# VectorE takes the maxima of pair t ahead of the scaling of pair t-1, and in the narrow attentions ScalarE alone copies the weights of both heads

## What is computed

```python
s = jnp.einsum('bqhd,bkhd->bhqk', q, k) * dh ** -0.5 + bias_or_mask
p = jax.nn.softmax(s, axis=-1)
o = jnp.einsum('bhqk,bkhd->bqhd', p, v)
```

## Time and profile before

| what | value |
|---|---|
| median of three runs | 1836.05 us (1833.36, 1836.05, 1836.85) |
| span of the profiled execution | 1837.6 us |
| TensorE busy | 1737.4 us, 95% of the span |
| VectorE busy | 1228.5 us, 67% |
| ScalarE busy | 1087.2 us, 59% |
| the chain that ended last | TensorE 80%, VectorE 9%, ScalarE 6%, issue 3%, DMA 2% |
| mean granted TensorE clock | 0.959 |

### The profile page before, as it was taken

How to read it: one execution, slowest core, us unless ns; L and a number is a source line. 1 busy time by engine, 2 the same in 40 slices (tenths; PEclk the granted TensorE clock), 3 DMA queues, 4 the chain that set the end, 5 groups by cost and what they waited for, 6 DMA issues and landing times.

```text
span 1837.6 us, 26822 instructions
## 1 busy us (share of the span) xinstructions
PE 1737.4 (95%) x9387; PEld 1436.8 (78%) x9387; DVE 1228.5 (67%) x1974; ACT 1087.2 (59%) x1682; POOL 14.1 (1%) x29
## 2 busy tenths in 40 slices
PE   5998999999999999999999999789999997989998
PEld 3875788888878767888888787578999875879997
DVE  3865588988968566888989555665455556555454
ACT  3535478888854454888887544555444546564443
POOL 1000000000000000000000000000000000000000
PEclk8998799999999998999999996899999999999999
DMA  9878569999967543899999443024655561225652
GB/s 346 295 276 305 206 239 337 384 320 346 381 232 274 174 148 138 322 340 366 360 335 372 145 155 115 24 92 139 202 186 177 161 225 48 89 95 184 196 190 71
DMA packets 217251, 413.06 MB, mean 225 GB/s; under 512 B 13088, under 2 KB 69456, under 8 KB 216768
## 3 DMA queue, kind: packets, MB, share of 16 engines
q1 hardware_dynamic: 214144, 400.74, 63.1%
q0 software_dynamic: 1904, 8.26, 1.5%
q10 hardware_dynamic: 1120, 2.97, 0.4%
HBM read 410.87 MB, written 1.05 MB: 224 GB/s over the span
## 4 chain that ended last, share of the span: by engine, by line
PE 80%; DVE 9%; ACT 6%; issue 3%; DMA 2%; SPq 0%; DVEq 0%; ACTq 0%
PE banks L774 22%; PE banks L775 21%; PE banks L776 21%; DVE weights_low L2203 3%; PE banks L946 2%; PE banks L804 1%; PE banks L905 1%; DMA weight_ring<-in_ada_w 1%; ACT scratch L1765 1%; ACT weights_high L1909 1%; PE banks L791 1%; PE banks L993 1%; PE banks L1007 1%; PE banks L1354 1%; PE banks L831 1%
## 5 line engine op out<-in xcount | busy, mean ns | idle before, releaser
L2203 DVE TENSOR_TENSOR weights_low<-weight_ring,weights_high 128x1024 fp32r<-128x1024 f32 (+1 forms) x656 | 771.2, 1217 | 183.7 <-ACT weights_high L1608 107.8
L774 PE MATMUL banks<-weights_high,features_parts 128*128 128x512 f32 (+1 forms) x1488 | 593.9, 399 | 16.0 <-DVE features_parts L2418 6.6
L775 PE MATMUL banks<-weights_low,features_parts 128*128 128x512 f32 (+1 forms) x1488 | 582.5, 391 | 0.0
L776 PE MATMUL banks<-weights_high,features_parts 128*128 128x512 f32 (+1 forms) x1488 | 582.2, 391 | 0.0
L1909 ACT ACTIVATE weights_high<-weight_ring 128x1024 fp32r<-128x1024 f32 x384 | 391.9, 1061 | 82.7 <-PE banks L776 50.5
L774 PEld LDWEIGHTS banks<-weights_high,features_parts 128*128 128x128 f32 x1488 | 282.5, 190 | 82.9 <-issue 15.3
L776 PEld LDWEIGHTS banks<-weights_high,features_parts 128*128 128x128 f32 x1488 | 281.8, 189 | 60.1
L775 PEld LDWEIGHTS banks<-weights_low,features_parts 128*128 128x128 f32 x1488 | 282.7, 190 | 55.3 <-issue 0.7
L1608 ACT ACTIVATE weights_high<-weight_ring 128x1024 fp32r<-128x1024 f32 (+1 forms) x176 | 176.9, 1044 | 140.0 <-PE banks L776 61.1
L774 PE MATMUL banks<-features_parts,weights_high 128*128 128x256 f32 x736 | 210.2, 286 | 2.1 <-DVE features_parts L2305 2.0
L775 PE MATMUL banks<-features_parts,weights_high 128*128 128x256 f32 x736 | 208.2, 283 | 0.0
(11 more groups left out here) (388 smaller groups left out, 1645.9 us busy)
## 6 DMA issues: line engine op xcount, KB each, us to landing
weight_ring<-in_exp_w_gate SPq DMA_DIRECT2D x128, 512.0 KB, 5.2
weight_ring<-in_exp_w_up SPq DMA_DIRECT2D x128, 512.0 KB, 5.1
weight_ring<-in_exp_w_down SPq DMA_DIRECT2D x128, 512.0 KB, 5.2
weight_ring<-in_ada_w SPq DMA_DIRECT2D x84, 512.0 KB, 5.9
weight_ring<-in_ffn_wg SPq DMA_DIRECT2D x44, 512.0 KB, 4.3
weight_ring<-in_ffn_wu SPq DMA_DIRECT2D x44, 512.0 KB, 4.7
weight_ring<-in_ffn_wd SPq DMA_DIRECT2D x44, 512.0 KB, 4.3
weight_ring<-in_even_w_in SPq DMA_DIRECT2D x28, 512.0 KB, 6.0
```

The source lines that it names most:

```text
L774: eng.matmul(dst, lh, rh, start=first, stop=False, **kw)
L775: eng.matmul(dst, lh, rl, start=False, stop=False, **kw)
L776: mm = eng.matmul(dst, ll, rh, start=False, stop=last, **kw)
L2203: V(half_of(low(s), i, size), half_of(slot(n), i, size), half_of(high(s), i, size).bitcast(F32), ALU.subtract)\
```

## The change

VectorE's step is put in another order: the maxima of pair t come first, then the reciprocals and the scaling of pair t-1. Its copy of the second head's transposed weights stays in the wide attentions only, right behind the scaling. In the narrow attentions ScalarE copies both heads in one instruction from banks 4 and 5, once both are transposed, and TensorE waits for this one copy. The wide attentions count VectorE's copies from zero (`first_wide`). TensorE's order of S, V and T is the same as before.

```diff
@@ class Pairs
+                self.first_wide = {"ca0": 0, "ca1": 2}.get(name, 0)
...
+            def turned_pair(self, t):
+
+                at = 1536 + 768 * (t % 2)
+                return SCRF[:, at:at + 768].rearrange("p (e n) -> p e n", e=2)
@@ TensorE: attention
-                        for e in range(2):
-                            eng.wait_ge(probs_copied[e], u + 1)
+                        eng.wait_ge(probs_copied[0], u + 1)
+                        if pairs.wide:
+                            eng.wait_ge(probs_copied[1], pairs.first_wide + t - 1)
...
-                            if t >= 2:
-                                eng.wait_ge(probs_copied[e], u)
+                            if t >= 2 and pairs.wide and e:
+                                eng.wait_ge(probs_copied[1], pairs.first_wide + t - 1)
+                            elif t >= 2:
+                                eng.wait_ge(probs_copied[0], u)
@@ ScalarE: attention
-                        eng.wait_ge(probs_turned, 2 * u + 1)
+                        eng.wait_ge(probs_turned, 2 * u + (1 if pairs.wide else 2))
                         if t >= 3 or (pairs.wide and t >= 2):
                             eng.wait_ge(values_ready, u if pairs.wide else u - 1)
-                        eng.activation(pairs.turned(t - 1, 0), B[4][:, 0:pairs.width], ACT.Copy)\
-                           .then_inc(probs_copied[0], 1)
+                        if pairs.wide:
+                            eng.activation(pairs.turned(t - 1, 0), B[4][:, 0:pairs.width], ACT.Copy)\
+                               .then_inc(probs_copied[0], 1)
+                        else:
+                            eng.activation(pairs.turned_pair(t - 1), PS[:, 4:6, 0:pairs.width], ACT.Copy)\
+                               .then_inc(probs_copied[0], 1)
@@ VectorE: attention
                 for t in range(n + 3):
+                    if t < n:
+                        for e in range(2):
+                            eng.wait_ge(scores_ready, 2 * (u0 + t) + e + 1)
+                            if t >= 2:
+                                eng.wait_ge(probs_turned, 2 * (u0 + t - 2) + e + 1)
+                            for tb in range(TB):
...
                     if 1 <= t <= n:
                         d, u, r = pairs.items[t - 1], u0 + t - 1, recips(t - 1)
...
                             ins.then_inc(probs_scaled, 1)
-                    if t < n:
...
-                    if 1 <= t <= n:
-                        u = u0 + t - 1
-                        eng.wait_ge(probs_turned, 2 * u + 2)
-                        if t >= 3 or (pairs.wide and t >= 2):
-                            eng.wait_ge(values_ready, u if pairs.wide else u - 1)
-                        eng.tensor_copy(pairs.turned(t - 1, 1), B[5][:, 0:pairs.width]).then_inc(probs_copied[1], 1)
+                        if pairs.wide:
+                            eng.wait_ge(probs_turned, 2 * u + 2)
+                            if t >= 2:
+                                eng.wait_ge(values_ready, u)
+                            eng.tensor_copy(pairs.turned(t - 1, 1), B[5][:, 0:pairs.width]).then_inc(probs_copied[1], 1)
```

More of the change, by code:

```diff
@@ L2383, in attention @@
                 for t in range(n + 3):
+                    if t < n:
[4 more added lines that the diff above has]
+                            for tb in range(TB):
+                                i, at = 2 * e + tb, pairs.score_cols(tb)
+                                eng.tensor_tensor_reduce(pairs.probs(t, e)[:, at], pairs.scores_bank(t, e)[:, at],
+                                                         pairs.items[t]["heads"][e]["masks"][tb], -pairs.scale, 3.0e38,
+                                                         ALU.add, ALU.min, small(SHIFT, t)[:, i:i + 1]).then_inc(shifted, 1)
                     if 1 <= t <= n:
@@ L2398, in attention @@
                             ins.then_inc(probs_scaled, 1)
-                    if t < n:
-                        for e in range(2):
-                            eng.wait_ge(scores_ready, 2 * (u0 + t) + e + 1)
+                        if pairs.wide:
+                            eng.wait_ge(probs_turned, 2 * u + 2)
                             if t >= 2:
[L2403 to L2408, removed]
-                    if 1 <= t <= n:
-                        u = u0 + t - 1
-                        eng.wait_ge(probs_turned, 2 * u + 2)
-                        if t >= 3 or (pairs.wide and t >= 2):
-                            eng.wait_ge(values_ready, u if pairs.wide else u - 1)
-                        eng.tensor_copy(pairs.turned(t - 1, 1), B[5][:, 0:pairs.width]).then_inc(probs_copied[1], 1)
+                                eng.wait_ge(values_ready, u)
+                            eng.tensor_copy(pairs.turned(t - 1, 1), B[5][:, 0:pairs.width]).then_inc(probs_copied[1], 1)
                     if t >= 3 and pairs.items[t - 3]["closes"]:
```

## The result

The changed kernel takes 1855.14 us (median of five executions, 1853.05 to 1856.62), the kernel before 1836.05 (five, 1833.36 to 1845.18): ratio 1.0085, 95% interval [1.0062, 1.0107]. Taken twice more, it gave 1852.79 and 1856.83 us, ratios 1.0087 in both. The forecast was 1842.0 with 1849.0 as its upper end: slower was right, the size was not.

What follows compares the result with a forecast made beforehand. The prediction took a loop of waits, with no engine full, to bound the attentions. Terms of +2.5 (a0), +5.0 (b0) and -1.7 us (ca0, ca1) sum to +5.8, hence 1842.0 us, range 1834.5 to 1849.

Steps and rivals of the forecast that it cites:

- the late starts in a0 and b0: Delays of TensorE's steps in attentions a0 and b0, forecast at +2.5 us and +5.0 us.
- a0: In attention a0, T(0) 1.7 us late and S(3) delayed about 1.1, partly hidden by loads: +2.5 us (+1.6 to +4).
- the clock's fall: In a0, the clock dropping once more, with nothing hidden by loads: the upper end, +4 us.
- What bounds the kernel: In the four attentions, no engine is full; a loop of waits (maxima, exponentials, scaling, maxima) sets the pace.
- The new loop: In b0's rounds, scaling(t) waits through T(t-1), S(t+1) and maxima(t+1): 3.98 us, taken as 3.9.
- The rounds of b0: Sparse pairs of b0, T(3) to T(10): each round grows by 0.35 us, seven rounds +2.5 us (+1.0 to +3.9).
- The head of b0: Start of b0: T(0) 2.0 us later, the next three pairs 0.4 each; +3.2 us (+2 to +4.5).
- The tail of b0: End of b0: V(10)'s wait for its copy shrinks, -1.0 us; a longer last copy adds 0.3.
- The joint copy: ScalarE's copy of 768 columns takes 0.8 us, is covered in b0's rounds, and adds 0.3 at b0's end.
- ca0 and ca1: Cross-attentions: V(0) starts 1.3 us earlier, part lost to the clock; -0.85 us each, -1.7 for both.
- The clock: Rival: idle TensorE in b0's rounds holds or brings back the low clock, rounds of 5.3 us, 1852 us; chance 0.06.

Runs made afterwards that it cites:

- the filled one: The changed kernel with seven products, results unused, put on TensorE between S(1) and T(0) of a0: 1850.43 us, ratio 1.0073.

## Why the prediction was wrong in size and right in sign

The distance to be explained is 15.3 us in the mean of three runs, against a forecast of 5.8. Of it 9.5 us stand at equal low-clock time, and 15.8 us more of the low clock make the rest: 0.37 x 15.8 = 5.8 us, which equals the forecast by chance alone. So two steps failed. The terms for the late starts in a0 and b0 were too small, by 3.7 us together (a0's order cost 4.5 us when taken out, with 2.5 forecast, b0's 6.6, with 5.0 forecast), and in a0 the clock's fall stood only at the upper end. And no term held more low clock in the program as a whole, which was put at nothing and measured at 5.8 us; its cause is open. The 9.5 comes from many executions; the single pair of profiles differs by 15.3 us at equal low-clock time, of which 4.3 us lie outside the attentions and are not explained.

- **What bounds the kernel: right.** A loop of waits set the pace. The new loop is the one forecast, in place and form: its sum was 3.98 us, and 4.03 was measured.
- **The rounds of b0: right in mechanism, undersized by 1.4 us.** From T(3) to T(10) the seven rounds took 28.16 us (1168.63 to 1196.79), and in the kernel before 24.24 (1150.92 to 1175.16): +3.9 in place of +2.5. Two things add up. I rounded my own 3.98 down to 3.9, on the guess that T's second half might run ahead; it did not (0.94 from T to S, and 4.02 a round): 0.9 us over seven rounds. The other 0.6 is a matter of where the rounds are counted. The old round of 3.55 us holds: the first maxima were 3.55 or 3.56 us apart six times in a row. But the old T's came by turns 2.9 and 4.2 us apart, and from T(3) to T(10) there are four short steps and three long ones (24.24 us, 3.46 a step). The sum of +3.9 is the upper end of the one stated. TensorE in the kernel before, the T's on both sides of the one at 1158.01:

```profile
1153.79 0.87 PE L1007 MATMUL banks<-constants,scratch 128*128 128x128 f32 x6
...
1160.93 0.88 PE L1007 MATMUL banks<-constants,scratch 128*128 128x128 f32 x6
```

- **The head of b0: undersized by 1.3 us.** T(0) came 1.96 us behind S(1)'s end, to a few hundredths as worked out. T(3), counted from S(0), came 37.80 us behind where it had been 33.28: +4.5 in place of +3.2. The three later pairs added 0.6 each and not 0.4, and 0.7 us arose before S(1) ended, where the changed kernel's execution had 1.4 us more of the low clock.
- **The tail of b0: right in sign, undersized.** From T(10) to the next projection 8.8 us in place of 10.4: -1.6 in place of -0.7.
- **The joint copy: right in its length, low in its price.** 0.81 us against 0.8. Over the kernel it cost 0.8 us by itself and 2.0 beside the new order, where I had put 0.3, for the end of b0 alone; the wait behind a0 grew as well, by 0.4 to 0.8 us.
- **a0: the first step that failed.** "T(0) is late by 1.7 us" held (1.65), but then I counted one more delay of 1.1 us, for S(3), and let the loads hide part. There are two, T(1) and T(2), each with a wait of 1.16 us at the full clock, and nothing hid them: 3.5 us of late starts, where the forecast had 2.5. In the changed kernel even the end of the stretch no longer waits for the loads. Worse, I put the clock into a0 as "if ... the clock drops once more, +4", an upper end. In the seven profiles with the new order there and the gap unfilled it dropped 6.8 to 8.1 us into a0, 0.2 to 1.3 us behind the start of T(0); in the filled one it did not, and of eight profiles with the old order one had a drop in the middle of a0, that of the kernel before, at 11.9 us. By the stretch a0 lost 5 to 8 us; the filled gap showed about half of the delay to be the clock's. At equal low-clock time of the whole program a0's order cost 3.3 us where it was put in alone and 4.5 where it was taken out.
- **ca0 and ca1: right.** -1.7 us forecast, -1.7 at equal low-clock time. In the changed kernel's own profile ca0 is 3.0 us shorter, as V(0) and V(1) also fell at the full clock.
- **The clock: the second step that failed, and its rival looked in the wrong place.** I looked for the low clock in the rounds, where gaps of 1.25 us left it at 1.00, and gave it 0.06. It entered as a larger sum over the whole program, which no term of mine held. I had read low-clock stretches off one execution as if they were fixed; 102 of them spread over 53 us of low clock, worth 20 us of time. My range of 14.5 us had no room for a shift of that mean.

**Open.** Why the mean of the low-clock time rises by 16 us with the changed kernel. Parts alone gave +3.4 (a0), +7.3 (b0), +1.0 (copy) and +0.5 (wide), 12.2 in sum, with errors of about 3 each; the 15.8 of the whole has an error of 3 to 4. Taken out of the changed kernel, b0's order took 10.5 us with it and a0's 0.8 (errors 4 to 5). So b0's order seems to bring most of it, perhaps with a part of the joint copy beside it. That b0's longer gaps do so was argued only: no kernel filled them.

## What to carry to other kernels

Before moving a step up in one engine's program, follow the loop through the other engines' program order: here the maxima came first on VectorE, but their scores still stood behind the transposes on TensorE, and the move paid only when TensorE's order was moved as well. Count a delay for every trip round the loop, and count the old rounds at the instructions at which the new ones will be counted, as one engine's steps can come by turns short and long. A gap opened on TensorE is priced twice, as waiting and as clock; where executions of one kernel spread widely in low-clock time, read that of many before calling a stretch's clock a fact.

## What the runs showed of the hardware

- The kernel before spent 117 to 170 us at 1.2 GHz from one execution to the next (102 executions), and each of these us went with 0.37 us of time (249 executions of all kernels, scatter 1.4 us).
- Gaps of 1.25 and 0.62 us by turns in rounds of 4.03 us left the granted clock at 1.00; a single gap of 1.96 us in a0 stood ahead of a fall to 0.50 in all seven profiles that had it unfilled, and with seven products of 128x512 in it (one profile) the clock stayed at 1.00. A single gap does not always do it: 2.12 us ahead of T(0) in ca0 left the clock at 1.00.
- ScalarE's copy of 128x768 from two PSUM banks took 0.81 us, against 0.47 for 128x384.
